# Four blocks of conditioning columns as products summed along the free dimension by VectorE, in the first layer's feed-forward

## The reference

```python
def modulation(cond, w_ada, b_ada):
    m = jax.nn.silu(cond) @ w_ada + b_ada          # (1024,) @ (1024, 6144)
    return [t[..., None, :] for t in jnp.split(m, 6, axis=-1)]
...
x = x + g1 * (mix(modulate(rms_norm(x, norm1_g[i]), sh1, sc1)) @ w_out[i])
x = x + g2 * conv_ffn(modulate(rms_norm(x, norm2_g[i]), sh2, sc2), w_up[i], conv_w[i], conv_b[i], w_down[i])
```

## Time and profile before

| | us |
|---|---|
| median of three runs | 1625.56 (1623.44 to 1626.12) |
| the profiled execution | 1623.06 |
| its span, first to last instruction | 1620.9 |
| PE busy | 1553.9 (96%) |
| DVE busy | 1055.0 (65%) |
| ACT busy | 839.4 (52%) |

### The profile page before, as it was taken

The page is one execution under the profiler, slowest core; times in us unless marked ns, Lnnn a source line. Parts: engine busy times, 40 slices in busy tenths (PEclk is TensorE's granted clock), DMA queues, the critical chain, the costliest instruction groups (busy, mean ns, idle before and its releaser), DMA issues.

```text
span 1620.9 us, 27655 instructions
## 1 busy us (share of the span) xinstructions
PE 1553.9 (96%) x9546; PEld 1279.1 (79%) x9546; DVE 1055.0 (65%) x1819; ACT 839.4 (52%) x1517; POOL 98.4 (6%) x152
## 2 busy tenths in 40 slices
PE   5999989999999999799899999999999999899997
PEld 3777667688888888697789998797788887588886
DVE  4443874756665477666678876754668865778865
ACT  4442872544444223455656655536556654566653
POOL 0111000000000111020000000020100001000000
PEclk9999999999999999999999999999999999799999
DMA  9765105332322587342177558442866688636663
GB/s 371 284 217 190 40 1 212 113 104 91 101 93 84 188 275 244 109 141 87 44 262 261 184 182 318 146 152 83 338 223 188 179 276 293 243 116 183 180 186 115
DMA packets 77091, 287.52 MB, mean 177 GB/s; under 512 B 8993, under 2 KB 12577, under 8 KB 67025
## 3 DMA queue, kind: packets, MB, share of 16 engines
q1 hardware_dynamic: 61056, 190.23, 37.2%
q0 software_dynamic: 15952, 96.18, 15.8%
HBM read 282.44 MB, written 1.05 MB: 175 GB/s over the span
## 4 chain that ended last, share of the span: by engine, by line
PE 81%; DVE 10%; issue 3%; ACT 3%; DMA 2%; DVEq 1%; SPq 0%; ACTq 0%
PE B L1810 15%; PE B L1811 15%; PE B L1812 15%; PE B L1827 11%; PE B L1825 6%; PE B L1847 3%; DVE WLO L1152 3%; PE B L2091 2%; PE B L1839 1%; PE B L1841 1%; PE B L1840 1%; PE B L2145 1%; PE B L1994 1%; DVE Y L1591 1%; PE B L2013 1%
## 5 line engine op out<-in xcount | busy, mean ns | idle before, releaser
L1152 DVE TENSOR_TENSOR WLO<-RAW,WHI 128x1024 fp32r<-128x1024 f32 (+1 forms) x376 | 412.1, 1099 | 168.7 <-ACT WHI L701 163.9
L701 ACT ACTIVATE WHI<-RAW 128x1024 fp32r<-128x1024 f32 (+1 forms) x376 | 358.4, 958 | 161.8 <-PE B L1812 90.7
L1810 PE MATMUL B<-HHL,WHI 128*128 128x256 f32 (+1 forms) x1168 | 395.7, 339 | 10.0 <-DVE HHL L1260 7.3
L1812 PE MATMUL B<-HHL,WLO 128*128 128x256 f32 (+1 forms) x1168 | 389.3, 333 | 0.0
L1811 PE MATMUL B<-HHL,WHI 128*128 128x256 f32 (+1 forms) x1168 | 389.2, 333 | 0.0
L1810 PEld LDWEIGHTS B<-HHL,WHI 128*128 128x128 f32 x1168 | 222.5, 190 | 48.8 <-issue 18.3
L1827 PE MATMUL B<-HHL,WHI 128*128 128x512 f32 x704 | 244.0, 399 | 3.6 <-DVE WLO L1152 1.9
L1812 PEld LDWEIGHTS B<-HHL,WLO 128*128 128x128 f32 x1168 | 222.6, 191 | 21.6
L1811 PEld LDWEIGHTS B<-HHL,WHI 128*128 128x128 f32 x1168 | 222.7, 191 | 20.2
L1825 PE MATMUL B<-HHL,WLO 128*128 128x256 f32 x704 | 184.0, 281 | 0.0
L1827 PE MATMUL B<-MID,WHI 128*128 128x512 f32 x462 | 162.6, 400 | 0.1
(11 more groups left out here) (237 smaller groups left out, 2170.5 us busy)
## 6 DMA issues: line engine op xcount, KB each, us to landing
RAW<-in_wup SPq DMA_DIRECT2D x176, 512.0 KB, 3.7
GWR<-in_wmod POOLq DMA_DIRECT2D x33, 1024.0 KB, 8.6
RAW<-in_wdn SPq DMA_DIRECT2D x64, 384.0 KB, 3.5
RAW<-in_wproj SPq DMA_DIRECT2D x44, 512.0 KB, 4.6
RAW<-in_wdn SPq DMA_DIRECT2D x64, 320.0 KB, 3.6
GWA<-in_wmod POOLq DMA_DIRECT2D x19, 1024.0 KB, 6.3
WINV<-in_wmod POOLq DMA_DIRECT2D x32, 512.0 KB, 5.6
...
```

The lines of the kernel that those rows point to most:

```text
L701: act_f(WH[s][:, 0:kts, :], RAW[s][:, 0:kts, :], ACT.Copy).then_inc(hi_done, 1)
L1152: v.tensor_tensor(WL[s][:, 0:kts, :], RAW[s][:, 0:kts, :], WH[s][:, 0:kts, :].bitcast(F32), ALU.subtract).then_inc(lo_done, 1)
L1810: mm(bank[:, 0:t], wh, a, start=first and k == ks[0], stop=False)
L1812: ins = mm(bank[:, 0:t], wl, a, start=False, stop=stop and k == ks[-1])
```

## The change

Groups 4, 5, 7 and 8 are now all made by DVE, and in another form. The weights of these groups are stored transposed (`wdot`), so that a piece of 128x1024 holds 128 output columns with all their 1024 rows along the free dimension; the conditioning vector (`c_2` for 7 and 8, `c` for 4 and 5) stands in all 128 partitions (`cbc`, two pieces of 512 KB, to which ACT applies silu). One DVE instruction multiplies a piece by that vector and sums it (`accum_out`) into one column of `DOT`; after 16 of them `DOT` is added to `MOD`. There are 64 pieces: 32 (groups 7 and 8) in `w_up(0)`, two per pair in the first 16 pairs, and 32 (4 and 5) in `w_down(0)`, at the places where `weigh` stood. The sums over partitions, the copies and the transposes of the four groups go. The DVE loop of `w_up(0)` is written out instead of looped. The units of group 9 move to the places of group 8, two units of group 10 to (2, "n2"), and no unit stands in (2, "n1"), in `proj(2)`, nor at the end of `w_up(2)`, `w_down(1)` and `w_down(2)`.

```diff
@@ -71,13 +71,18 @@
-         7: "H0 H1 H2 H3 R6 A R8 A", 8: "A K0 K1 R5 R6 R8 R9 R10", 9: "A K0 K1 R6 R8 R9 R10 A",
-         10: "H0 H1 H2 H3 R6 A R8 R9", 11: "R10 R6 A R8 R9 R10 R6 A"}
+         9: "A K0 K1 R5 R6 R8 R9 R10", 10: "A R6 H0 H1 H2 H3 R8 R9", 11: "R10 R6 A R8 R9 R10 R6 A"}
-WEIGHED = [4, 5]
+DOTS = [7, 8, 4, 5]
@@ -211,9 +216,12 @@
+        CB = [sb(f"CB{k}", [P, D], at=gwat + 4096 * k) for k in range(2)]
+        WDOT = [[sb(f"WDU{b}", [P, D], at=at) for b, at in enumerate(
+            [w0 + 32768 + 4096 * b for b in range(3)] + [w0 + 77824 + 4096 * b for b in range(3)])],
+            [sb(f"WDD{b}", [P, D], at=hhat + 4096 * b) for b in range(6)]]
+        DOT = DER[:, 2].rearrange("p a b -> p (a b)")
@@ -582,11 +590,13 @@
+            def fetch(n):
+                if n >= 6:
+                    gp.wait_ge(dotted, n - 5)
+                gp.dma_start(WDOT[n // 32][n % 32 % 6][:], A["wdot"][P * n:P * n + P, :]).then_inc(
+                    wdot_ready[n % 32 % 6], 16)
@@ -646,14 +654,17 @@
+            gp.wait_ge(gw_used, unit_index(3, 0) + 1)
+            for k in range(2):
+                gp.dma_start(CB[k][:], A["cbc"][P * k:P * k + P, :]).then_inc(cb_in, 16)
+            gp.wait_ge(gw_used, unit_index(3, 7) + 1)
+            for n in range(32):
+                fetch(n)
             gp.wait_ge(blk_used, DOWN0[0])
...
+            for n in range(32, 64):
+                fetch(n)
@@ -664,24 +675,18 @@
-            for kt in range(7):
-                gp.wait_ge(blk_used, DOWN0[1] + 4 * kt)
-                unit(7, kt)
...
-            gp.wait_ge(blk_used, UP0[2] + 4)
-            for kt in range(4, 8):
-                unit(9, kt)
+            for kt in range(2):
+                unit(10, kt)
             gp.wait_ge(blk_used, DOWN0[2])
-            for kt in range(8):
-                gp.wait_ge(blk_used, DOWN0[2] + min(4 * kt, 24))
+            for kt in range(2, 8):
+                gp.wait_ge(blk_used, DOWN0[2] + 4 * kt - 8)
                 unit(10, kt)
@@ -768,10 +770,6 @@
-                if key == (1, "n1"):
-                    row_out(4)
-                elif key == (2, "n1"):
-                    act.wait_ge(gw_used, unit_index(7, 3) + 1)
@@ -1055,6 +1053,10 @@
                 warm(ACT.Silu)
+                if l == 0:
+                    act.wait_ge(cb_in, 32)
+                    for k in range(2):
+                        act_f(CB[k][:], CB[k][:], ACT.Silu).then_inc(cb_silu, 1)
@@ -1253,8 +1256,6 @@
-                    if key == (1, "n1") and kt == 0:
-                        dve.wait_ge(wsum_mm, 2)
@@ -1629,6 +1630,9 @@
                             lo_split(n4 + 1, s0 + 1, DOWN_KT[s0 + 1] if last else 8)
+                        if l == 0 and pair < 16:
+                            dot(2 * pair)
+                            dot(2 * pair + 1)
                         dve.wait_ge(mid_hi, pg + 1)
@@ -1638,20 +1642,27 @@
+                ins = v.scalar_tensor_tensor(out=t[:], in0=t[:], scalar=1.0, in1=CB[n // 32][:], op0=ALU.mult,
+                                             op1=ALU.mult, accum_out=DOT[:, k:k + 1])
+                ins.then_inc(dotted, 1)
+                if k == 15:
+                    dve.wait_ge(dotted, n + 1)
+                    m = MOD[:, 16 * g:16 * g + 16, 0]
+                    link(v.tensor_tensor(m, m, DOT, ALU.add))
+                    link(v.memset(DOT, 0.0))
@@ -1675,11 +1686,11 @@
-                                        weigh(n)
+                                        dot(32 + n)
@@ -1968,18 +1969,16 @@
-                if key == (1, "n1"):
-                    weighed_sum(5)
-            FILL_ROOT = {(0, "n2"): (3, [4]), (1, "n2"): (6, [0]), (2, "n1"): (7, [2]), (2, "p1"): (8, [2]), (2, "p2"): (10, [2])}
-            FILL_SPREAD = {(0, "n2"): (3, [5, 6, 7]), (1, "n2"): (6, [1, 2, 3, 4]), (2, "n2"): (9, [0, 1, 2, 3]), (2, "n1"): (7, [3, 4]), (2, "p1"): (8, [3, 4, 5, 6, 7]),
+            FILL_ROOT = {(0, "n2"): (3, [4]), (1, "n2"): (6, [0]), (2, "p1"): (9, [2]), (2, "p2"): (10, [2])}
+            FILL_SPREAD = {(0, "n2"): (3, [5, 6, 7]), (1, "n2"): (6, [1, 2, 3, 4]), (2, "p1"): (9, [3, 4, 5, 6, 7]),
+                           (2, "n2"): (10, [0, 1]), (2, "p2"): (10, [3, 4, 5, 6, 7]), (3, "n1"): (11, [0, 1, 2, 3]),
@@ -2070,12 +2069,10 @@
-                    if (l, i) in ((0, 10), (1, 3), (1, 8), (2, 10)):
-                        mod_turn({(0, 10): 1, (1, 3): 4, (1, 8): 5, (2, 10): 7}[l, i])
+                    if (l, i) == (0, 10):
+                        mod_turn(1)
-                    if l == 2 and i in (2, 4, 7):
-                        mod_unit(7, {2: 5, 4: 6, 7: 7}[i])
@@ -2322,8 +2319,8 @@
-                if l in (1, 2):
-                    fill(*((6, [5, 6, 7]) if l == 1 else (9, [4, 5, 6, 7])))
+                if l == 1:
+                    fill(6, [5, 6, 7])
@@ -2343,15 +2340,11 @@
-                            if l < 3 and isinstance(i, int) and i == 0 and a == 0 and s == 2:
-                                mod_turn((3, 6, 9)[l])
+                            if l < 2 and isinstance(i, int) and i == 0 and a == 0 and s == 2:
+                                mod_turn((3, 6)[l])
-                if l == 0:
-                    weighed_sum(4)
-                elif l < 3:
-                    fill((7, 10)[l - 1], [0, 1])
```

More of the change, by code:

```diff
@@ L264, in build @@
         gw_ready = {k: sem(f"gw_ready_{k}") for k in GW}
-        winv_ready = [sem(f"winv_ready{b}") for b in range(6)]
-        weighed_v, wsum_mm = sem("weighed_v"), sem("wsum_mm")
+        wdot_ready = [sem(f"wdot_ready{b}") for b in range(6)]
+        cb_in, cb_silu, dotted = sem("cb_in"), sem("cb_silu"), sem("dotted")
         gw_used, gb_done, gb_ev, sel_done, mod_add = (sem("gw_used"), sem("gb_done"), sem("gb_ev"), sem("sel_done"),
@@ L620, in proj @@
                 for i in range(NSLOT[l]):
-                    if l == 2 and i == 3:
-                        unit(7, 7)
                     if l == 0 and 1 <= i < 15:
@@ L789, in norm @@
                         late_squares(key, c)
-                        if key in TURNED and c == {8: 2, 11: 0}.get(TURNED[key]):
+                        if key in TURNED and c == {9: 2, 11: 0}.get(TURNED[key]):
                             row_out(TURNED[key])
@@ L1903, in mod_unit @@
                 if kt == 0:
[L1904 removed]
+                    pe.wait_ge(gb_ev, turn_place(g))
                 mod_kt(kt, GW[HOME[u]]).then_inc(gw_used, 1)
[L1907 to L1915 removed]
             def fill(g, kts):
```

91 lines of the change are left out of this document (34 added, 57 removed).

## The result

The changed kernel takes 1613.87 us (median of seven runs, 1610.73 to 1617.89); the kernel before, on the same chip, took 1623.98 (1619.80 to 1626.12). The ratio is 0.9946, with a 95% interval of 0.9931 to 0.9960: 8.8 us faster by that ratio, give or take 2.4 (the two medians differ by 10.1). Two more measurements of the same kernel gave 1615.95 and 1613.17 us, ratios 0.9948 and 0.9935. The forecast was 1613.1 us. That it lies only 0.8 us from the measured time is partly luck: it started from three executions of the kernel before with the median 1625.56 us, and from the seven now at 1623.98 us the same sum would have given 1611.5 us. The gain came out nearer 9 or 10 us than the 12.5 us of the sum, and most of what follows is about the cause.

What follows compares the result with a forecast made beforehand. PE was taken as the bound, busy 96% of the span. Six terms sum to 13.4 us gained, less 0.9 for the clock: 12.5 us off the 1625.56 us median gives 1613.1 us, range 1609 to 1620.

Steps and rivals of the forecast that it cites:

- The new work: DVE's dots in `w_up(0)` and `w_down(0)`: 1.35 us each, hidden behind PE, cost nothing; added transfers cost nothing.
- Rival (a): Dots run at half rate, 2.56 us, and DVE becomes the bound in `w_up(0)` and `w_down(0)`: 1647 us, chance 0.10.
- Rival (b): Dots nearly too long, or the start of `w_up(0)` too tight: some 4 us of PE waits, 1617 us, chance 0.11.
- Terms 1 and 2: Three units removed from `proj(2)` gain 3.0 us; four transposes removed in `proj(1)`, `proj(2)` and `w_down(2)` gain 1.7 us.
- term 6: In (2, n1), the root's spread no longer waits behind a running unit: 0.4 us gained.
- the clock: With filling gone from (2, n1), PE idles and its clock falls into the products: 0.9 us lost, at most 1.7.
- One of my signs of being wrong: Forecast is wrong if products at half clock show up in more than one of the norms.
- Term 4: In (2, n2), two units instead of four let products start earlier, then paced by DVE: 3.5 us gained (2.9 to 4.3).
- Rival (c): Clock falls more often in (1, n1), (2, n1), (2, n2): 5 us lost instead of 0.9, 1617 us, chance 0.09.
- Terms 3 and 5: Four units gone from the end of `w_up(2)`: 2.9 us (to 3.6); four 1 MB loads gone from its start: 1.9 us.
- Rival (d): DVE paces the start of `w_up(2)` and gives back 5.4 us of gain: 1618.5 us, chance 0.05.
- the end of `w_up(2)`: what is late next: First product of `w_down(2)` waits for DVE to drain a bank, so 2.9 of 3.6 us are gained.

Runs made afterwards that it cites:

- a0_again: The changed kernel once more, unchanged, against the kernel before: a gain of 6.8 us by the medians.
- x3: Changed kernel plus five units of idle matmuls in each of (1, n1) and (2, n1): median 2.2 to 4.9 us lower than the changed kernel's, ratio interval 0.9898 to 0.9950.
- x7: Changed kernel with three of group 10's loads in `w_up(2)`, four others spread over `w_down(2)`, and five idle units in each of (1, n1) and (2, n1): 1609.15 us.
- b0_after: The changed kernel unchanged, as yardstick for three runs on the same chip, against the kernel before: a gain of 10.3 us.
- x1_small_loads: Changed kernel with the seven 1 MB conditioning loads beside `w_down(2)` each moving a quarter of its bytes: 1607.23 us against 1615.95 for the changed kernel.
- x2_filled_end: Changed kernel plus four units of idle matmuls at the end of `w_up(2)`: 1612.56 us against 1615.95 for the changed kernel.

## Why the forecast was right, and where its sum was not

**The new work: right.** The dot was put at 1.35 us and is 1.30 listed; from one start to the next it is 1.15, as a listed end overlaps the next start. It costs nothing: from the first product of `w_up(0)` to the first of `proj(1)` the kernel took 369.3 us before and 369.3 after. Rival (a) is out. The Trainium skill's rule, "Vector Engine (DVE) Microarchitecture Reference", section 7, is that such an instruction on two sources from SBUF that aren't bf16 runs at half throughput. It does not show here: 1219 ns with the accumulator in use is what the weight split over as many elements takes (1.22 us), not twice that. Rival (b) is out too: PE has no wait for weights in `w_up(0)`. The doubled dots show the cover there and its end. Transfers and silu (1.04 us each) are free, as costed.

**Terms 1 and 2: right; term 6 and the clock: right within 1 us.** The two transposes of `proj(1)` show where the same low stretches occur in both kernels: 166.08 us from `proj(1)`'s first product to `w_up(1)`'s before, 165.24 after in a0_again, 0.84 less for 0.86. From the first product of `proj(2)` to the last of `w_out(2)` it was 124.5 us before and is 121.1 in x3 and x7, which have no low clock there: 3.4 us, exactly three units and a transpose. In the changed kernel 0.7 to 1.4 us of that come back, at the low clock; I had put 0.9. Term 6, 0.4 us, doesn't show: from the last product of `w_down(1)` to the first of `proj(2)` it was 7.7 us before and is 8.4, 7.8 and 7.3 in the three profiles. From the last product of `w_down(1)` to the last of `w_out(2)` all these terms together gain 2.0, 1.9 and 2.9 us (132.2 before) for 2.9 in the sum. The Trainium skill's warning ("TensorE: Matmul & The Clock Gate", section on HAM oscillation) and the trace agree, with 0.50 where the earlier trace rows has 1.00.

One of my signs of being wrong did appear: products at half clock in more than one norm. From 664 to 670 us, where `proj(1)` starts, the granted clock is 0.50 and was 1.00 before, and in the first profile the first products of `proj(2)` and of `w_up(2)` run at it too. At `proj(1)` that costs nothing (369.3 us as before), as DVE is busy all of these 6 us in both kernels; the sign took half clock for lost time.

**Term 4, (2, n2): short.** I had DVE pace the products as soon as PE had done two units. But these ran partly or wholly at the low clock and held the first product. Timeline of PE and DVE after, against the earlier trace rows:

```profile
1163.19 1.94 PE L1858 MATMUL B<-GWA,CV 128*32 128x512 f32 x8
1164.90 1.94 PE L1858 MATMUL B<-GWR,CV 128*32 128x512 f32 x8
...
1166.77 0.80 PE L1838 MATMUL B<-HHL,WHI 128*128 128x512 f32 x1
...
1169.76 0.48 DVE L1261 SCALAR_TENSOR_TENSOR HHL<-NORM,MOD,HHL 128x256 fp32r<-128x256 f32 x1 [0.18 <-ACT HHL L780]
```

Two units take 3.6 us here (3.2 and 3.0 in the other two profiles) instead of 2, and DVE's last block is there well before PE has its pair of tiles. From the spread to the 48th product it was 14.8 us before, 12.8, 11.9 and 11.7 after: 2.0 to 3.2 us gained for 3.5 (2.9 to 4.3). In some executions the stretch ahead of it, (2, p1), is longer as well. In the third profile ACT's split of a weight of `w_up(2)`, ahead of the norm's work in its queue, waited for its transfer, the squares were queued behind it, and PE stood before the norm's sum (timeline of ACT and PE, then a window behind it):

```profile
1150.43 1.06 ACT L706 ACTIVATE WHI<-RAW 128x1024 fp32r<-128x1024 f32 x1 [1.79 <-DMA RAW<-in_wup]
...
1154.72 0.61 PE L1937 MATMUL B<-CST,ACC 128*128 128x1 f32 x4 [1.51 <-DVE ACC L1543]
```

```profile
1156.60:1160.60 4.00, 4.00 (x25) 1.15 (x28) 3.81 (x7) 2.12 (x3) 0.20 (x1) 0.57 0.52 214
```

After that the clock is low (0.57 in this window) while PE does the five units of that norm, and from the last product of `w_out(2)` to the first of `w_up(2)` it takes 19.8 us where the other two profiles have 17.3 and 16.8 (19.6 before). With that, term 4 gains nothing in this profile. Rival (c) is thus half true: low stretches come and go. Where PE has work throughout they cost some 1.5 us each: from the first product of `proj(1)` to that of `w_up(1)` the same code took 165.2 us with two more of them in a0_again, 163.6 with one in b0_after and 162.1 with none in the first profile. The profile of the kernel before has two such stretches, so some 3 us of what the first profile gained are no doing of the change. They are a good part of the scatter between executions.

**Terms 3 and 5: right, at the upper ends.** From the first product of `w_up(2)` to the first of `w_down(2)` it is 5.1 to 5.6 us shorter for 2.9 + 1.9 = 4.8. The end of it after, against the earlier trace rows:

```profile
1291.21 0.42 DVE L1592 TENSOR_TENSOR Y<-B,Y 128x256 f32<-128x256 f32 x1
...
1291.29 0.39 PE L1838 MATMUL B<-HHL,WHI 128*128 128x512 f32 x1
...
1291.68 0.50 PE L1838 MATMUL B<-MID,WHI 128*128 128x512 f32 x1
```

The next stage starts with no gap behind the last product. DVE drains the bank at 1291.21 to 1291.63, just in time. Rival (d) does not occur: no PE wait for DVE in `w_up(2)`, and no term is given back there.

**What failed is the step "the end of `w_up(2)`: what is late next".** I looked for the next thing late at the first product alone, found a bank, and took `w_down(2)` itself as unchanged but for a transpose. It is 2.8 to 5.8 us longer, where the transpose should have made it 0.4 shorter. The loads beside it make its weights late (x1_small_loads), and the four units had been filling and also a head start of 3.6 us (x2_filled_end) for a stage that runs its transfers at 307 GB/s before (273 after), with a 1 MB load beside each tile. The change also moved the loads that go out together to a place 7 us earlier in that stage, at which the forecast did not look; what this adds stays open. The sum of 12.5 us less some 5 for this, less 1 on term 4 and plus 0.6 on terms 3 and 5, is 7 us, against 8.8 measured (6.8 to 10.3 by the three pairs of medians). What is between them is within the scatter by the clock, and I can't divide it further. My range had room for the loss; my reasons had not. That 12.5 us of gain from a high median before and 10 from a lower one land on nearly the same time is luck.
